# Attention order of both layers, small transfers, heads scaling, router order and the order of the last gate

## The chip, the cores and the metric

The kernel runs on one core of a Trainium2 chip. The metric is the device time of one execution in microseconds (us). Five instruction streams run beside each other on the core and meet only at semaphores: TensorE (PE, matrix products into the banks of PSUM), VectorE (DVE), ScalarE (ACT), GpSimd (POOL) and SyncE (SP). Sixteen DMA engines move data; DMAs are issued by SP, ACT and POOL, each through a queue of its own. An engine takes its instructions strictly in program order, so a wait holds back all that stands behind it on the same engine.

## The reference

A two-layer block with adaptive shifts, scales and gates, then a second block with a convolution, a linear recurrence, a router with 32 experts and a gate. 256 tokens, 1024 features, float32.

```python
def first_block(x, c, ...):
    for l in range(DEPTH):                         # 2 layers
        ada = jax.nn.silu(c) @ w_ada[l] + b_ada[l]
        sh1, sc1, g1, sh2, sc2, g2 = jnp.split(ada, 6)
        h = x * (1.0 + sc1) + sh1
        y = mixer_ab(...) if l % 2 == 0 else mixer_cd(...)
        x = layer_norm(DEEPNORM_ALPHA * x + (1.0 + g1) * y, ...)
        h = x * (1.0 + sc2) + sh2
        y = swiglu(h, w_ffn_in[l], w_ffn_out[l])
        x = layer_norm(DEEPNORM_ALPHA * x + (1.0 + g2) * y, ...)

def mixer_ab(h, ...):    # 4 heads with two softmax maps each, then 8 dilated heads
    p = softmax(s0) - lam_full * softmax(s1); oa = p @ va
    oa = oa * lax.rsqrt(jnp.mean(jnp.square(oa), -1, keepdims=True) + LN_EPS)
    oa = oa * subln_g * (1.0 - lambda_init)
    ob = dilated_attention(qb, kb, vb, ...)
    return jnp.concatenate([oa, ob], axis=-1) @ w_o

def second_block(x, p, ...):
    x = x + jnp.concatenate([y_conv, y_lru], axis=-1) @ w_out
    hf = _rmsnorm(x, g_ffn)
    eid, gate = _hier_route(hf, ...)               # best group of 4, then its 2 best of 8 experts
    x = x + _routed_experts(hf, eid, gate, w1, w3, w2)
    e = _rmsnorm(p @ w_ple, g_ple_proj)
    x = x + jax.nn.sigmoid(_rmsnorm(x, g_ple) @ w_ple_gate) * e
    return _rmsnorm(x, g_final)
```

## The kernel before

Weights of the first block and of the second one's mixers come as units of 1 MB (`w_raw`, five slots, issued by SP in order by `load_unit`, L457; each waits until PE is done with the unit five earlier). ACT splits each unit into a high part and DVE into the rest (`w_parts`, L1424 and L1971), so that a float32 product is made of three reduced ones (L740, L743, L747; in the attention L795, L797, L799). The vector `ada` comes from 48 further pieces of 1 MB (`aring`, two slots, issued by POOL, L628), each multiplied and summed on DVE in two instructions (`piece`, L1954).

The attention of a layer is eight steps j on PE: the queries and keys of step j, then `beat(j-2)`: the scores of pair j-2, the outputs of pair j-4, and the transposes of the probabilities of pair j-3 (`pair_probs`). After that come the last beats, interleaved with the output projection `from_heads`. On DVE a beat is shift (add bias, mask, minimum), the split of a unit, then the normalising of two probability tiles. In layer 0, pairs 0 to 3 are heads with two maps, whose two softmax tiles are mixed into one (`normalise`, L2076 to L2080). Their outputs land in PSUM bank 6, two heads at a time. ACT squares them (`head_squares`) and takes the root (`head_deviation`), DVE inverts it and multiplies the outputs out of PSUM (`scale_heads`, L2087 and L2090). PE transposes them (`heads_t`), ACT copies and rounds them (`take_heads`), DVE makes the rest (`heads_low`). PE waits for `head_scaled` before it writes output 2 over bank 6.

POOL's queue is in program order too: pieces, the bias bands of maps 8 to 15 (four DMAs, L652), the first row of gates written to DRAM element by element (`gate_out(0)`, L634) and read back as a row for 128 partitions (`gate_back(0)`, L638). The input `x_tm` (1 MB) is loaded by SP behind unit 13 (L504); its first use is `ln_half` (L2130). WO_AT is 12 and FF_AT is 16: units 12 to 15 are those of the output projection, 16 is the first of the feed-forward part.

The router is a chain over three engines: residual sum (L2531), multiplication by g_ffn (L2534), 16 transposes on PE (L1218), 32 products with `w_route` (L1229), then one link after another on DVE: two softmax parts, the two largest of 32, the gates (L2580 to L2589), the ranks of the tokens within their expert from five products (L1264 to L1268), the slots (L2602). Products that add zeros (`scatter`, L1247) stand between on PE. Then the 16 pairs of experts run, with 6 MB of weights each through slots in SBUF. Behind the last pair the results are scattered back (L1247), summed (L2657), transposed (L1365), and multiplied by the gate's weights `pg_parts` in four units (high parts L1377 and L1389, low parts L1382); sigmoid, product and final norm follow, and two stores of 512 KB from SP (L611).

## Time and profile before

| | us |
|---|---|
| median of 3 runs | 1271.91 |
| lowest, highest | 1270.47, 1273.64 |
| profiled execution, whole | 1268.73 |
| its span | 1266.9 |

The profile shows one execution, 3.2 us shorter than the median, with 1.8 us of its time outside the span. Times of rows are in us from the start of the span. On its axis: layer 0's attention until 144, its feed-forward part until 350, layer 1's attention 395 to 465, the mixers of the second block until 765, the router until 789, the experts until 1229, and the end. In a row of the timeline a bracket tells how long the engine was idle before it, and what ended that.

### The profile page before, as it was taken

Reading aid. Unit: us, or ns where it says so; the run is one execution under the profiler, and the core shown is the slowest. Engines: PE = TensorE matmul, PEld = TensorE weight load, DVE = VectorE, ACT = ScalarE, POOL = GpSimd, SP = SyncE. Lnnn points to the kernel's source line nnn. Section 1 sums busy time; section 2 is a strip of 40 time slices with the busy share of each in tenths; the row PEclk is TensorE's granted clock in tenths of the full one; section 3 lists DMA queues with packets and bytes.
Section 4 is the critical chain, followed back from the end, with each engine's and each line's share of the span. In section 5 each row is a group of like instructions: output and inputs, shape, how many; then the busy total and the mean of one; then the engine's idle time right before and its main releaser. Section 6 shows DMA issues by size and latency. Waiting matters only on the chain.

```text
span 1266.9 us, 16567 instructions
## 1 busy us (share of the span) xinstructions
PE 1207.7 (95%) x6608; PEld 833.4 (66%) x6608; DVE 668.0 (53%) x1194; ACT 501.1 (40%) x745; POOL 54.7 (4%) x102
## 2 busy tenths in 40 slices
PE   6997899999899999999999999999999999999987
PEld 2686678878789877888877787444544444454436
DVE  5598968687779786664468476111111111111127
ACT  1476563434475566343445375111111111111135
POOL 0111000000000000101001200000000000000000
PEclk9998999999999999999999999999999999999999
DMA  9998658988746545757556769999999999999990
GB/s 368 386 314 274 255 203 324 301 318 325 275 189 221 200 171 197 312 209 212 199 199 224 242 261 397 386 413 426 427 426 424 426 425 427 426 427 424 426 412 36
DMA packets 49035, 396.02 MB, mean 313 GB/s; under 512 B 6257, under 2 KB 7473, under 8 KB 10450
## 3 DMA queue, kind: packets, MB, share of 16 engines
q1 hardware_dynamic: 38610, 337.69, 67.7%
q0 software_dynamic: 9568, 56.55, 12.8%
q10 hardware_dynamic: 800, 0.99, 0.2%
...
## 4 chain that ended last, share of the span: by engine, by line
PE 72%; DMA 12%; DVE 10%; ACT 3%; issue 2%; SPq 1%; DVEq 0%; POOL 0%; ACTq 0%
PE psum L1295 16%; PE psum L740 9%; PE psum L747 8%; PE psum L743 8%; PE psum L1336 8%; PE psum L1239 4%; DMA slabs<-in_w 3%; DMA aring<-in_ada 3%; PE psum L1247 3%; DMA w_raw<-in_units 3%; DVE aring L1954 3%; DVE w_parts L1971 2%; DMA staged<-in_ada 2%; PE psum L795 1%; PE psum L1026 1%
## 5 line engine op out<-in xcount | busy, mean ns | idle before, releaser
L1971 DVE TENSOR_TENSOR w_parts<-w_raw,w_parts 128x2048 fp32r<-128x2048 f32 x106 | 242.1, 2288 | 92.6 <-ACT w_parts L1424 92.6
L1424 ACT ACTIVATE w_parts<-w_raw 128x2048 fp32r<-128x2048 f32 x106 | 202.0, 1911 | 104.4 <-DMA w_raw<-in_units 104.4
L1295 PE MATMUL psum<-slabs,arena 128*64 128x512 f32 x896 | 223.0, 593 | 2.8 <-issue 2.6
L740 PE MATMUL psum<-w_parts,h_parts 128*128 128x512 f32 x416 | 165.1, 397 | 4.2 <-ACT h_parts L1424 2.0
L743 PE MATMUL psum<-w_parts,h_parts 128*128 128x512 f32 x416 | 162.3, 390 | 0.0
L1295 PEld LDWEIGHTS psum<-slabs,arena 128*64 128x64 f32 x896 | 73.1, 137 | 112.1 <-issue 110.0
L1424 ACT ACTIVATE arena<-psum 128x512 f32<-128x512 f32 (+1 forms) x59 | 33.3, 567 | 272.6 <-PE psum L1309 140.9
L747 PE MATMUL psum<-w_parts,h_parts 128*128 128x512 f32 x416 | 111.5, 390 | 0.0
L1954 DVE CUSTOM_DVE_ANT_0 aring<-aring,cb 128x1024 f32<-128x1024 f32 x80 | 94.6, 1219 | 4.7 <-DMA aring<-in_ada 4.6
L740 PEld LDWEIGHTS psum<-w_parts,h_parts 128*128 128x128 f32 x416 | 78.1, 188 | 22.6 <-DVE act_tm L2167 3.4
L747 PEld LDWEIGHTS psum<-w_parts,h_parts 128*128 128x128 f32 x416 | 78.1, 188 | 16.5
L743 PEld LDWEIGHTS psum<-w_parts,h_parts 128*128 128x128 f32 x416 | 78.2, 188 | 15.5
L1938 DVE SCALAR_TENSOR_TENSOR y_lo<-psum,slot_gate,y_hi 128x512 fp32r<-128x512 f32 x32 | 24.0, 751 | 102.8 <-ACT y_hi L1424 102.8
L740 PE MATMUL psum<-w_parts,act_ring 128*128 128x512 f32 x176 | 69.6, 395 | 4.3 <-issue 2.8
L743 PE MATMUL psum<-w_parts,act_ring 128*128 128x512 f32 x176 | 69.2, 393 | 0.0
L795 PE MATMUL psum<-h_parts,w_parts 128*128 128x256 f32 x256 | 64.7, 290 | 0.0
L797 PE MATMUL psum<-h_parts,w_parts 128*128 128x256 f32 x256 | 63.2, 284 | 0.0
L1239 PE MATMUL psum<-arena,resid_tm 128*128 128x128 f32 x512 | 59.9, 275 | 0.0
L1424 ACT ACTIVATE y_hi<-psum,slot_gate 128x512 fp32r<-128x512 f32 x32 | 22.0, 687 | 93.2 <-PE psum L1336 93.2
L1239 PEld LDWEIGHTS psum<-arena,resid_tm 128*128 128x128 f32 x512 | 58.4, 192 | 0.3 <-DVE arena L2602 0.3
L1336 PE MATMUL psum<-arena,arena 128*64 128x512 f32 x256 | 56.7, 595 | 0.0
L1336 PE MATMUL psum<-w_odd,arena 128*64 128x512 f32 x256 | 56.7, 595 | 0.0
...
## 6 DMA issues: line engine op xcount, KB each, us to landing
...
```

Source lines behind the costliest of these rows:

```text
L740: mm(psum[:, bank, :], high(tile, tok), w_hi(k)[:, col:col + 512], start=first and bank not in begun, stop=False, skip_group_check=True)
L743: mm(psum[:, bank, :], high(tile, tok), w_lo(k)[:, col:col + 512], start=False, stop=False, skip_group_check=True)
L747: ins = mm(psum[:, bank, :], low(tile, tok), w_hi(k)[:, col:col + 512], start=False, stop=done, skip_group_check=True)
L795: mm(half(j % 2, s), w_hi(k)[:, at_(kt)], h_hi[:, kt, :], start=kt == 0 and s == 0, stop=False, skip_group_check=True)
L797: mm(half(j % 2, s), w_lo(k)[:, at_(kt)], h_hi[:, kt, :], start=False, stop=False, skip_group_check=True)
L1239: last = nc.tensor.matmul(psum[:, bank_no, k * P:(k + 1) * P], hf_t(t, kt), hot_s[:, t, :, :], start=t == 0, stop=t == TT - 1)
L1247: last = nc.tensor.matmul(psum[:, 4 + 2 * t + c, :], hot_gt[:, t * P:(t + 1) * P], part[:, c * 512:(c + 1) * 512], start=start and n == 0, ...
L1295: ins = nc.tensor.matmul(psum[s * CAP:(s + 1) * CAP, w, :], xe_t[:, kt, s * CAP:(s + 1) * CAP], up_weights(w, s, b, kt), start=kt == 0, st ...
L1336: ins = nc.tensor.matmul(psum[s * CAP:(s + 1) * CAP, c, :], act_t[:, f, s * CAP:(s + 1) * CAP], w2_at[b][:, c * 4096 + s * 2048 + f * 512: ...
L1424: return nc.scalar.activation(out_ap, in_ap, func, **kw)
L1954: v.tensor_tensor_reduce(out=w, in0=w, in1=cb[:], scale=1.0, scalar=0.0, op0=ALU.mult, op1=ALU.add, accum_out=ada_raw[:, 2 * slot + t:2 * ...
L1971: v.tensor_tensor(w_lo(k), raw(k), w_hi(k).bitcast(F32), ALU.subtract).then_inc(w_split, 1)
```

## The change

Both layers' attention: on PE the transposes of the probabilities of pair j-3 move from the inside of the beat to behind the products of step j; on ACT the copies of these tiles move with them. In layer 0 each head's output gets a half bank of its own in banks 6 and 7, and the output of head 2 no longer waits for `head_scaled`; the first transposes of heads move from beat 4 to behind step 6. DVE only inverts the roots (`head_factors`); ACT multiplies the heads (`scale_heads`). The mix of two maps is written with one map left without its own denominator, and the root takes a bias per head and token, which makes four roots of one column out of one of four. The bands of maps 8 to 15, `gate_out(0)` and `gate_back(0)` are issued by ACT, and POOL issues pieces 8 to 21 without anything between. `x_tm` is loaded behind unit 17. In both layers pairs 4 and 5 are rounded on ACT ahead of exponentials.

Router: g_ffn is multiplied into `w_route` earlier in the program; PE transposes the sum itself; the five products for the ranks read rounded operands (`tri_r`, `ones_r`, `both_r`); ahead of them stand 8 wide and 16 narrow products with zeros, where 24 wide ones stood; the gates are computed after the slots and after the number of rounds is signalled.

End: half of the last scatter moves into the last expert's second products, high and low parts of the gate's products are interleaved differently, DVE makes all four halves of the sum before the low weights, and spreads the latter between the low parts of the sum; the table for the sigmoid is loaded earlier, the one for the last root without a call of its own; the last chunk is squared on DVE; ACT stores tile 0.

```diff
@@ SP
-                if k == WO_AT + 1:
+                if k == FF_AT + 1:
                     sp.dma_start(x_tm[:], a["x_rows"]).then_inc(x_in, 16)
@@ POOL
             bands(0, 4)
-            pieces(8, 10)
-            pieces(10, 12)
-            pool.wait_ge(bias_in, BANDS)
-            bands(8, 16)
-            pieces(12, 14)
-            gate_out(0)
-            pieces(14, 16)
-            gate_back(0)
-            pieces(16, 22)
+            pieces(8, 22)
@@ PE, attention
-                if i == 2:
-                    pe.wait_ge(head_scaled, 1)
-                elif i:
+                if i % 2:
                     pe.wait_ge(head_squared, i)
...
+                    if j >= 3:
+                        pair_probs(layer, j - 3)
+                    if layer == 0 and j == 6:
+                        heads_t(0)
@@ PE, router
-            for _ in range(3):
-                for c in range(2):
-                    scatter(c, True, False)
-
-            pe.wait_ge(route_d, 3)
+            for c in range(2):
+                scatter(c, True, False)
+            for n, part in enumerate((y_hi, y_lo)):
+                for k in range(8):
+                    nc.tensor.matmul(psum[:, 4 + k // 4, k % 4 * P:k % 4 * P + P], hot_gt[:, 0:P], part[:, k * P:(k + 1) * P],
+                                     start=False, stop=False, skip_group_check=True)
+
+            pe.wait_ge(route_d, 2)
@@ ACT, attention
+            def scale_heads(n):
+
+                act.wait_ge(head_rooted, head_rooted_from + n + 1)
+                for i in (2 * n, 2 * n + 1):
+                    for t in range(TT):
+                        col = head_col(i, t)
+                        ins = A(o_tm[:, i, t, :], head_bank(i)[:, t * P:(t + 1) * P], Cp, scale=head_sq[:, 2, col:col + 1])
+                ins.then_inc(head_scaled, 1)
...
+            def first_gate_back():
+                act.wait_ge(first_gate, first_gate_from + 16)
+                act.dma_start(g_row[:], bass.AP(gate_rows.tensor, 0, [[0, P], [1, D]])).then_inc(first_gate, 16)
...
                     split(u + QK_AT + j + 3)
+                    if layer == 0 and j == 5:
+                        scale_heads(0)
+                    if layer == 0 and j == 2:
+                        bands(8, 16)
+                    elif layer == 0 and j == 7:
+                        first_gate_out()
@@ DVE, normalise of a head with two maps
-                    link(v.reciprocal(den[:, m0:m + 1, :], den[:, m0:m + 1, :]))
-                    link(v.tensor_scalar(den[:, m, :], den[:, m, :], small[:, 14:15], None, ALU.mult))
-                    v.tensor_scalar(s1[:, 0:256], s1[:, 0:256], den[:, m, 0:1], None, ALU.mult)
-                    link(v.tensor_scalar(s1[:, 256:384], s1[:, 256:384], den[:, m, 1:2], None, ALU.mult))
-                    stt(s[:, 0:256], s[:, 0:256], den[:, m0, 0:1], s1[:, 0:256], ALU.mult, ALU.add)
+                    stt(head_sq[:, 3, m0:m0 + 2], den[:, m0, :], LN_EPS, den[:, m0, :], ALU.mult, ALU.mult)
+                    link(v.reciprocal(den[:, m, :], den[:, m, :]))
+                    link(stt(den[:, m, :], den[:, m, :], small[:, 14:15], den[:, m0, :], ALU.mult, ALU.mult))
+                    stt(s[:, 0:256], s1[:, 0:256], den[:, m, 0:1], s[:, 0:256], ALU.mult, ALU.add)
@@ DVE, heads
-            def scale_heads(n):
+            def head_factors(n):
 
                 dve.wait_ge(head_std, n + 1)
-                link(v.reciprocal(head_sq[:, 2, 4 * n:4 * n + 4], head_sq[:, 1, 4 * n:4 * n + 4]))
-                for i in (2 * n, 2 * n + 1):
-                    for t in range(TT):
-                        ins = v.tensor_scalar(o_tm[:, i, t, :], psum[:, 6, (i % 2) * T + t * P:(i % 2) * T + (t + 1) * P],
-                                              head_sq[:, 2, 2 * i + t:2 * i + t + 1], None, ALU.mult)
-                ins.then_inc(head_scaled, 1)
+                v.reciprocal(head_sq[:, 2, 4 * n:4 * n + 4], head_sq[:, 1, 4 * n:4 * n + 4]).then_inc(head_rooted, 1)
@@ DVE, router: the gates' operations (nine) move behind this line
+            v.tensor_copy(rounds_i[:], r_s[:, 12, 0:1]).then_inc(routed, 2)
@@ DVE, end
             summed(0, 0)
+            summed(1, 0)
+            gate_low(0, 0)
             summed(0, 1)
-            gate_low(0, 0)
+            summed(1, 1)
+            pg_low(0)
             gate_low(0, 1)
-            pg_low(0)
             pg_low(1)
-            summed(1, 0)
-            summed(1, 1)
             pg_low(2)
@@ ACT, end
+            table_of_sigmoid()
...
-            table_of_sqrt()
             token_root("final", 0)
```

PE in layer 0's attention, before: the scores of a pair (L822), the output of head 2 (L875 to L877), the transposes of scaled heads (L884), the transposes of probabilities (L840 to L842).

```order
L822 MATMUL psum<-qk 128x256 [waits qk_taken,score_rd]
L822 MATMUL psum<-qk 128x256
L822 MATMUL psum<-qk 128x128 x2
L875 MATMUL psum<-val,prob_t 128x128 [waits head_scaled,pt_copied]
L876 MATMUL psum<-val,prob_t 128x128
L877 MATMUL psum<-val,prob_t 128x128
L884 MATMUL psum<-cst,o_tm 128x128 [waits head_scaled]
L884 MATMUL psum<-cst,o_tm 128x128 x3
L840 MATMUL psum<-cst,score 128x128 [waits pt_copied,prob_ready]
L841 MATMUL psum<-cst,score 128x128
L842 MATMUL psum<-cst,score 128x128
```

The same place after, from the last row of the scores on; L803 and L805 are the products of step 6:

```order
L830 MATMUL psum<-qk 128x128 x2
L879 MATMUL psum<-val,prob_t 128x128 [waits pt_copied]
L880 MATMUL psum<-val,prob_t 128x128
L881 MATMUL psum<-val,prob_t 128x128
L803 MATMUL psum<-h_parts,w_parts 128x256
L805 MATMUL psum<-h_parts,w_parts 128x256
```

PE after, at the end of step 6, with the transposes of probabilities (L848 to L850) and of heads (L888):

```order
L805 MATMUL psum<-h_parts,w_parts 128x256
L807 MATMUL psum<-h_parts,w_parts 128x256 x8
L848 MATMUL psum<-cst,score 128x128 [waits pt_copied,prob_ready]
L849 MATMUL psum<-cst,score 128x128
L850 MATMUL psum<-cst,score 128x128
L888 MATMUL psum<-cst,o_tm 128x128 [waits head_scaled]
L888 MATMUL psum<-cst,o_tm 128x128 x3
L803 MATMUL psum<-h_parts,w_parts 128x256 [waits qk_taken,w_split]
```

The output of head 2 lost its wait for `head_scaled`, and both kinds of transposes moved from the beat to behind step 6's products, the heads behind the probabilities.

ACT in layer 0's attention, before, from the last `take_qk` to the last exponentials (line 1424 is the helper of all activations):

```order
L1424 ACTIVATE qk<-psum 128x512
L1424 ACT_TABLE_LOAD
L1424 ACTIVATE head_sq<-head_sq,small 128x4
L1424 ACTIVATE w_parts<-w_raw 128x2048
L1424 ACTIVATE o_whole<-psum,small 128x512
L1424 ACTIVATE o_parts<-o_whole 128x512
L1424 ACT_TABLE_LOAD
L1424 ACTIVATE score,den<-score,mins 128x256
```

ACT after, the same place (helper in line 1449):

```order
L1449 ACTIVATE qk<-psum 128x512
L1449 ACTIVATE prob_t<-psum 128x384 x2
L1449 ACT_TABLE_LOAD
L1449 ACTIVATE head_sq<-head_sq 128x1 x4
L1449 ACTIVATE o_tm<-psum,head_sq 128x128 x4
L1449 ACTIVATE w_parts<-w_raw 128x2048
L1594 DMA gate_rows<-drv 128x8x1
L1449 ACTIVATE o_whole<-psum,small 128x512
L1449 ACTIVATE o_parts<-o_whole 128x512
L1449 ACTIVATE o_parts<-psum 128x256
L1449 ACT_TABLE_LOAD
L1449 ACTIVATE score,den<-score,mins 128x256
```

PE at the end, before, from the last expert's second products (L1336) to the transposes of the sum (L1365); `y_hi` and `y_lo` are the parts of the last expert's result:

```order
L1336 MATMUL psum<-w_odd,arena_81 64x512 x7
L1354 REGISTER_ALU
L1247 MATMUL psum<-y_hi,hot_gt 128x512 [waits y_low0,sgt_c]
L1247 MATMUL psum<-y_lo,hot_gt 128x512
L1247 MATMUL psum<-y_hi,hot_gt 128x512
L1247 MATMUL psum<-y_lo,hot_gt 128x512
L1247 MATMUL psum<-y_hi,hot_gt 128x512 [waits y_low1]
L1247 MATMUL psum<-y_lo,hot_gt 128x512
L1247 MATMUL psum<-y_hi,hot_gt 128x512
L1247 MATMUL psum<-y_lo,hot_gt 128x512
L1365 MATMUL psum<-cst,x_tm 128x128 [waits x_ready]
L1365 MATMUL psum<-cst,x_tm 128x128 x3
```

PE after, the same place:

```order
L1359 MATMUL psum<-w_odd,arena_81 64x512 [waits w2_loaded11]
L1359 MATMUL psum<-w_odd,arena_81 64x512 x3
L1356 REGISTER_ALU
L1264 MATMUL psum<-y_hi,hot_gt 128x512 [waits y_low0,sgt_c]
L1264 MATMUL psum<-y_hi,hot_gt 128x512
L1264 MATMUL psum<-y_lo,hot_gt 128x512 [waits y_low0]
L1264 MATMUL psum<-y_lo,hot_gt 128x512
L1359 MATMUL psum<-w_odd,arena_81 64x512 x4
L1381 MATMUL psum<-cst,x_tm 128x128 [waits x_ready,y_low0]
L1381 MATMUL psum<-cst,x_tm 128x128 x3
L1259 REGISTER_ALU
L1264 MATMUL psum<-y_hi,hot_gt 128x512 [waits y_high]
```

Four scatter products moved into the second products (L1359), and the first transposes (L1381) ahead of the other four.

## Rows read from the trace of the kernel before

**Rows 1.** The page: span, and busy tenths of PE in 40 slices.

```profile
span 1266.9 us, 16567 instructions
...
PE   6997899999899999999999999999999999999987
```

**Rows 2.** The page: the chain that ended last, shares by engine.

```profile
PE 72%; DMA 12%; DVE 10%; ACT 3%; issue 2%; SPq 1%; DVEq 0%; POOL 0%; ACTq 0%
```

**Rows 3.** Timeline of PE, layer 0's attention: start, busy us, line, what, idle before.

```profile
99.66 0.76 PE L875 MATMUL psum<-val,prob_t 128*128 128x128 f32 x2 [5.07 <-DVE o_tm L2090]
```

**Rows 4.** Windows there: busy us (instructions) of PE, PEld, DVE, ACT, POOL; clock, DMA share, GB/s.

```profile
102.00:104.00 2.00, 2.00 (x12) 2.00 (x11) 1.54 (x4) 2.00 (x9) 0.00 (x0) 0.55 0.10 8
104.00:106.00 2.00, 2.00 (x19) 2.00 (x19) 1.76 (x4) 1.37 (x4) 0.00 (x0) 1.00 0.89 57
...
136.00:138.00 2.00, 2.00 (x13) 1.72 (x12) 1.97 (x4) 1.94 (x4) 0.53 (x1) 1.00 0.00 0
```

**Rows 5.** Timeline of DVE, layer 0's attention and the start of its norm.

```profile
93.90 1.23 DVE L1954 CUSTOM_DVE_ANT_0 aring<-aring,cb 128x1024 f32<-128x1024 f32 x1 [1.62 <-DMA aring<-in_ada]
...
96.86 0.35 DVE L2078 TENSOR_SCALAR score<-score,den 128x256 f32<-128x256 f32 x1
...
98.39 1.13 DVE L2090 TENSOR_SCALAR o_tm<-psum,head_sq 128x128 f32<-128x128 f32 x4
...
109.91 0.42 DVE L2059 CUSTOM_DVE_ANT_0 score<-psum,bias 128x256 f32<-128x256 f32 x1 [2.48 <-PE psum L822]
...
132.74 0.42 DVE L2102 TENSOR_TENSOR o_parts<-psum,o_parts 128x256 fp32r<-128x256 f32 x1 [1.64 <-ACT o_parts L1424]
...
144.43 0.68 DVE L2130 TENSOR_TENSOR ln_tmp<-psum,g_row 128x512 f32<-128x512 f32 x1
```

**Rows 6.** Timelines of ACT and POOL, and landing times of the DMAs on the gates' rows.

```profile
130.57 0.51 ACT L1424 ACTIVATE score<-score,mins 128x256 f32<-128x256 f32 x1 [3.42 <-DVE mins L2061]
...
74.65 2.36 POOL L652 DMA_DIRECT2D bias<-bias_rows  x4
...
DMA to landing us min/median/max: 8.9/10.0/14.1
```

**Rows 7.** Timeline of SP: unit 17's issue; landing times of the weights from 100 to 160.

```profile
139.24 0.33 SPq L461 DMA_DIRECT2D w_raw<-in_units  x1
...
DMA to landing us min/median/max: 4.7/7.4/12.4
```

**Rows 8.** Timeline of PE, layer 1's attention.

```profile
439.61 0.47 PE L740 MATMUL psum<-w_parts,o_parts 128*128 128x512 f32 x1 [0.73 <-issue]
```

**Rows 9.** Timelines of PE and DVE in the router.

```profile
771.18 1.26 PE L1218 MATMUL psum<-cst,resid_tm 128*128 128x128 f32 x8 [1.11 <-DVE resid_tm L2534]
...
788.89 4.51 PE L1295 MATMUL psum<-slabs,arena 128*64 128x512 f32 x20
...
781.59 0.16 DVE L2580 TENSOR_REDUCE arena<-arena 128x2 f32<-128x8 f32 x1
...
783.56 0.20 DVE L2591 TENSOR_SCALAR arena<-arena 128x64 f32<-128x64 f32 x1
```

**Rows 10.** The chain in the last experts, and a window in the first.

```profile
1188.73 22.34 DMA slabs<-in_w
...
792.00:794.00 2.00, 2.00 (x12) 0.67 (x10) 0.00 (x0) 0.00 (x0) 0.00 (x0) 1.00 0.76 250
```

**Rows 11.** Timelines of PE, DVE, ACT and SP at the end.

```profile
1234.80 1.16 PE L1377 MATMUL psum<-pg_parts,g_hi 128*128 128x512 f32 x4 [1.26 <-ACT pg_parts L1424]
...
1235.93 4.87 DVE L1938 SCALAR_TENSOR_TENSOR pg_parts<-slabs,vec,pg_parts 128x1024 fp32r<-128x1024 f32 x4
...
1258.96 1.28 ACT L1424 ACT_TABLE_LOAD   x1
1260.26 0.20 ACT L1424 ACTIVATE small<-small 128x1 f32<-128x1 f32 x1
...
1262.55 0.82 SPq L611 DMA_DIRECT2D out<-resid_tm  x2
```

373 lines of the change are left out of this document (214 added, 159 removed).

## The prediction

> **What bounds the kernel now.** I read the page first: PE is busy in nearly every slice [rows 1], and the chain of waits is 72% PE, with 12% DMA and 10% DVE [rows 2]. So an edit pays only where PE, or what it waits for, comes late on that chain. The timeline then says where. In layer 0's attention the chain runs through DVE: PE stood 5.07 us before it could write output 2, because DVE was still scaling heads [rows 3], and came back at a low clock. From 102 to 104 the granted clock was 0.55 and PE did 12 instructions; in the next 2 us, at 1.00, it did 19 [rows 4]. DVE itself had few gaps: 1.62 us on a piece, 2.48 on scores, 1.64 on ACT [rows 5]. Its last link is the start of the first norm at 144.43 [rows 5]. Layer 1's attention has one gap worth the name, 0.73 us [rows 8]. In the router PE waits 1.11 us for the gain, and the first expert product starts at 788.89 [rows 9]. The last experts end on DMAs: 22.34 us of chain for one slab [rows 10]. The end is PE, then a table load, a root and two stores from one queue [rows 11].
>
> **Layer 0's attention.** What DVE loses: four scalings of heads, 1.13 us, twice, with the reciprocals staying, so 2.26 us; and in each of four mixes one pass of 0.35 us over a tile, 1.4 us in all [rows 5]. That is 3.7 us off an engine that is on the chain. What the freed PE gains is more, 5.07 us and about 1.5 us of half clock (23 instructions in 4 us of which 19 fit into 2 us, less what the clock gave back), but PE then runs into DVE. I carried this through: scores of pair 5 move from 109.91 to about 102, since the gap of 2.48 and part of the 1.62 go with PE's stall; behind them the lead shrinks, because DVE now works without a gap and waits for roots and for ACT's scaled heads instead. ACT's four scalings have a cover: ACT was idle 3.42 us in one place of this stretch [rows 6]. The norm starts 4.2 us earlier by this, just above the 3.7 us. The bounds: 1.0, if DVE meets new waits for nearly all that it lost, and 9.4, if the 3.7 us and all three gaps (5.74 us) go.
>
> Against it stands `x_tm`. SP now issues it behind unit 17, whose issue came at 139.24 [rows 7]. That issue waits for PE, so it moves with the lead to 135.0, and `x_tm` follows at about 135.4. The norm would need it at 140.2. The DMA engines had a hole from 136 to 138 [rows 4], and the weights of this stretch landed after 4.7 us at best, 7.4 in the middle, 12.4 at worst [rows 7]. The best gives 140.1 and no wait, the middle 142.8 and 2.6 us, the worst 147.8 and 7.6 us. I take 1.0, nearer the best because of the hole. Before, `x_tm` was loaded long ahead and cost nothing.
>
> **Small transfers.** Four bands, which took POOL 2.36 us to issue [rows 6], now take ACT's time behind the split of step 2. There ACT waited for DVE, so I price them at nothing; without that cover it is 2.4 us. `gate_out(0)` is issued at about 114 and lands 8.9 to 14.1 us later [rows 6], at 123 to 128. ACT reaches the wait for it at about 123, and its next exponentials would be free at 126.4 (130.57 less 4.2), so its idle 3.42 us hide a landing up to 12.4 us after issue. The worst row leaves 1.7 us. Queued behind that wait are the rounding of pair 5 and two tiles' exponentials, for which DVE and PE wait. I take 0.3. POOL's pieces no longer stand behind these transfers, but the piece that DVE waited 1.62 us for was held by its free slot and its landing, so I give the move nothing. The stage's sum is 4.2 - 1.0 - 0.3 = 2.9 us, between -5.7 (the lead at 1.0, `x_tm` at its middle, bands and gates uncovered) and 9.4.
>
> **Layer 1's attention.** The order of transposes fills the gap of 0.73 us [rows 8]; DVE loses nothing here. 0.5 us, between 0 and 1.
>
> **Router.** PE's 1.11 us before the second transposes go, since the gain is off the chain; I take 1.0. The nine linked gate operations between 781.59 and 783.56 [rows 9], 1.97 us, leave the way to the slots, but PE's products for the ranks stand there too, so that about 1.4 us come through. The first expert product moves from 788.89 to 786.5, 2.4 us. It is not worth that at the end: the experts end on DMAs [rows 10], so only what fills the dip in the first of them counts. From 792 to 794 the DMA engines were busy 0.76 of the time [rows 10], so about 0.5 us of transfer was missed there. An earlier start of the experts shortens that hole and what lies beside it. I take 1.2, between 0.5 and 2.4.
>
> **End.** Scatter products inside the second products take away the shadow in which nothing else was ready; PE's 1.26 us before the gate's first product [rows 11] shrink by half. But DVE must now make four sums, four low parts of the sum and eight passes of 1.22 us over low weights (4.87 us for four [rows 11]) without a gap: 8 passes over 512 columns at 0.68 [rows 5] and 9.7 us are 15.1 us from about 1232, so the last low weights are there at 1247, where PE asks for them. I take 0.7 us of loss on PE. Behind the last product the table load of 1.28 us [rows 11] starts 0.3 us earlier, and the stores, issued 0.4 us apart by one queue (0.82 us for both [rows 11]), come from two queues together: 0.5 us of gain. Sum: -0.2 us, between -1.5 and 1.5.
>
> Table loads have a second price. On the chain at the end, ACT's table load took 1.28 us, and the next activation started 0.02 us behind it [rows 11]. The Trainium skill ("ScalarE: Activation LUTs", "What ACT_TABLE_LOAD costs") adds a drain of 1.38 us to each switch. By the page, hiding the loads of the router and of the sigmoid would give 2.8 us more, and the sum would be 7.2 us; the trace shows no drain, and I go by the trace.
>
> **Sum.** 2.9 + 0.5 + 1.2 - 0.2 = 4.4 us. The profiled execution took 1268.73 us, so it would take 1264.3. The median is 3.2 us above the profiled execution; the forecast is 1267.5. A measurement of this kernel can tell about 0.3%, 3.8 us, from no change, that is less than 1268.1 is faster and more than 1275.7 slower.
>
> **Rivals.**
> Forecast, 0.50: DVE's lost work comes through, 1263.5 to 1270.
> More, 0.17: the gaps of DVE go with its work. Layer 0 gives 9.4 - 1.3 = 8.1, layer 1 0.5, the router its whole 2.4, the end 0: 11.0 us, 1260.9. For it: PE's stall was the cause of the 2.48. Against: each gap has a different releaser, and DMAs end the experts.
> DVE stays the clock, 0.20: PE's idle time only moves, from output 2 to the wait for `prob_ready`, since the transposes now stand ahead of step j+1; layer 0 gives 1.0, the router 0.5, the end costs 0.5: 1.0 us, 1270.9. This is also how it would look if the order did not do what it says.
> Late `x_tm`, 0.13: at its worst landing, the first norm starts at 147.8, 3.4 us later than before, and PE stands for that time, as all of DVE's queue is behind that wait. With 0.5, 1.2 and -0.2 of the others that is 1.9 us slower, 1273.8. It decides from a landing of 9.0 us after issue: then the norm starts where it did.
>
> **How the numbers follow.** The likeliest case gives 1267.5. The range 1260.5 to 1273.5 leaves out about half of the last rival, the low side of the second, and little of the others, under 2 in 10. Faster by over 0.3%: 0.42 of the forecast's 0.50 and the second's 0.17, 0.59. Slower: 0.10, the last rival with a transfer later than seen, or a stage at its lower bound. Same: the rest, 0.31.
>
> **What would show it.** Right: no idle time of PE on scaled heads; clock 1.00 from 100 to 104; first norm at 140 to 142; first expert product at 786 to 787; last product of the gate about 1 us later than the shift of the rest. Wrong: an idle DVE before the norm that ends on `x_tm`; ACT idle on the gates' rows ahead of exponentials; PE idle on low weights at the end; a first expert product 2.4 us nearer and an end that gained it all.

## The result and the profile after

| | before | after |
|---|---|---|
| median of 4 runs each, us | 1271.85 | 1263.93 |
| lowest, highest | 1270.47, 1273.64 | 1262.62, 1265.41 |
| profiled execution, whole | 1268.73 | 1264.81 |
| its span | 1266.9 | 1263.0 |

The ratio of the medians is 0.9933, with a 95% interval from 0.9911 to 0.9956: 7.9 us faster. The two profiled executions differ by 3.9 us only. Before's lies 3.1 us below its median, after's 0.9 above its own. So the profiles can place a gain, but they can't be summed to the medians. The experiments show later why.

The page of the kernel after: its span, the busy tenths of PE, and the shares of the chain. They answer to [rows 1, 2].

```profile
span 1263.0 us, 16569 instructions
...
PE   6998899999899999999999999999999999999987
...
PE 74%; DMA 11%; DVE 9%; ACT 3%; issue 1%; SPq 1%; DVEq 0%; POOL 0%; ACTq 0%
```

PE's share of the chain rose from 72% to 74%; DMA and DVE each lost a point.

**Layer 0's attention.** Timelines of PE and DVE after, four rows with idle time from 60 to 142 us. They answer to [rows 3, 5].

```profile
108.42 0.77 PE L748 MATMUL psum<-w_parts,o_parts 128*128 128x512 f32 x1 [2.47 <-issue]
...
135.66 0.79 PE L755 MATMUL psum<-w_parts,o_parts 128*128 128x512 f32 x1 [2.23 <-DVE o_parts L2172]
...
123.54 0.43 DVE L2172 TENSOR_TENSOR o_parts<-psum,o_parts 128x256 fp32r<-128x256 f32 x1 [2.20 <-ACT o_parts L1449]
...
139.69 0.69 DVE L2200 TENSOR_TENSOR ln_tmp<-psum,g_row 128x512 f32<-128x512 f32 x1 [1.89 <-PE psum L755]
```

The stall of 5.07 us before output 2 is gone, and no PE row waits for a scaled head. About half of it came back at another place: at 108.42 PE waits 2.47 us before the first product of the output projection. The view names no releaser, but this product waits for `qk_taken` (L905), and ACT's last copy of queries and keys ended at 108.32. That copy stands in ACT's order behind exponentials, and ACT had been idle 2.89 us for DVE's minima ahead of them. In the experiments below this wait is there with 2.46 to 2.48 us in every kernel that has the attention of the change without an edit. At 135.66 PE waits another 2.23 us for the low part of a head's output on DVE. The first norm starts at 139.69 instead of 144.43, 4.7 us earlier. The windows of 2 us of the kernel after, with the columns of [rows 4]:

```profile
102.00:104.00 2.00, 2.00 (x19) 2.00 (x19) 1.97 (x6) 0.72 (x5) 0.53 (x1) 1.00 0.40 168
...
108.00:110.00 2.00, 1.58 (x4) 1.32 (x5) 1.93 (x7) 1.98 (x4) 0.00 (x0) 0.50 0.91 356
...
136.00:138.00 2.00, 2.00 (x6) 1.52 (x6) 1.80 (x1) 1.82 (x1) 0.10 (x1) 0.50 1.05 438
...
160.00:162.00 2.00, 2.00 (x6) 1.62 (x5) 1.80 (x2) 2.00 (x5) 1.73 (x4) 0.50 0.19 49
```

The last three columns are clock, DMA share and GB/s. From 102 to 104 the clock is 1.00, as predicted. But it is 0.50 at three other places, the first of them right behind the wait of 2.47 us; it may fall there in one execution and not in the next (below). From 136 to 138 the DMA engines are now full, where before they stood still [rows 4].

**`x_tm` and the gates' row.** Timelines of SP and ACT after, with the landing time of `x_tm`. They answer to [rows 6, 7].

```profile
131.55 0.43 SPq L522 DMA_DIRECT2D x_tm<-in_x_rows  x1
...
DMA to landing us min/median/max: 8.1/8.1/8.1
...
111.49 0.39 ACTq L1594 DMA_DIRECT2D gate_rows<-drv  x1
...
123.13 0.38 ACT L1449 ACTIVATE o_parts<-psum 128x256 fp32r<-128x256 f32 x1 [1.45 <-DMA gate_rows<-drv]
```

`x_tm` was issued at 131.55 and its landing was seen 8.1 us later, at 139.65. The norm starts there. The view puts DVE's 1.89 us down to PE, but that product had ended at 138.94; the last 0.7 us are the transfer's. The norm also waits for `x_tm` in every other execution whose `x_tm` stands behind unit 17, eleven in the experiments below: it landed 8.1 or 8.2 us after its issue in all of them, and the norm started within 0.1 us of the landing. DVE was idle 1.9 to 2.0 us there, and PE's product had ended 0.7 to 2.2 us before. It had ended late in the execution above, since the clock was 0.50 from 136 to 138. So 0.7 us is the low end of what the transfer costs. ACT waits 1.45 us for the gates' row, and behind it DVE waits the 2.20 us for `o_parts` shown above.

**Router.** PE after: transposes, ranks, first expert product, against [rows 9].

```profile
766.74 2.20 PE L1221 MATMUL psum<-cst,x_tm 128*128 128x128 f32 x16
...
777.81 0.28 PE L1284 MATMUL psum<-both_r,tri_r 128*128 128x32 f32 x1 [1.74 <-DVE both_r L2649]
...
783.22 1.08 PE L1315 MATMUL psum<-slabs,arena 128*64 128x512 f32 x4
```

The transposes begin 2.3 us earlier than before (769.04), the first expert product 5.7 us earlier than in [rows 9]. So the router gained 3.4 us in this pair of traces, a pair in which the clock fell behind the transposes before and not after. All of it arrives: the second products of the last expert pair start at 1216.50 instead of 1222.24, 5.7 us earlier. The DMAs at [rows 10] didn't hold it back.

**End.** PE and DVE after, behind the last second products, and a window of the same place. They answer to [rows 11].

```profile
1225.67 0.75 DVE L2015 SCALAR_TENSOR_TENSOR y_lo<-psum,slot_gate,y_hi 128x512 fp32r<-128x512 f32 x1 [3.94 <-ACT y_hi L1449]
1226.34 1.27 DVE L2729 TENSOR_TENSOR x_tm<-x_tm,psum 128x512 f32<-128x512 f32 x2
1227.17 0.72 PE L1381 MATMUL psum<-cst,x_tm 128*128 128x128 f32 x4 [2.26 <-DVE x_tm L2729]
...
1228.00:1230.00 2.00, 2.00 (x6) 1.54 (x6) 1.45 (x3) 2.00 (x3) 0.00 (x0) 0.50 0.41 168
...
1253.58 1.12 PE L1405 MATMUL psum<-pg_parts,g_hi 128*128 128x256 f32 x8
```

Here is a new wait. PE transposes the sum of the first half, and that sum stands in DVE's order behind the low part of the second half of `y`, which comes late: PE is idle 2.26 us and then has the low clock. From the start of the second products to the end of the gate's last product it takes 38.2 us (1216.50 to 1254.70), before 35.8 us (1222.24 to 1258.04). Behind the last product the rest takes 8.3 instead of 8.9 us. Timelines of ACT and SP there:

```profile
1255.22 1.28 ACT L1449 ACT_TABLE_LOAD   x1
1256.52 0.48 ACT L1449 ACTIVATE rms<-rms,small 128x1 f32<-128x1 f32 x2
...
1258.60 0.37 ACTq L2000 DMA_DIRECT2D out<-resid_tm  x1
...
1258.60 0.34 SPq L628 DMA_DIRECT2D out<-resid_tm  x1
```

The two stores now leave together.

### The profile page after: what moved, and what is told of

Read it like the earlier page. It is cut to its first block, busy times and chain, and to the rows that moved or that the text cites. A ratio compares the mean times of both kernels' runs of the same rounds, so it can differ in the third digit from the quotient of the medians.

```text
span 1263.0 us, 16569 instructions
## 1 busy us (share of the span) xinstructions
PE 1207.7 (96%) x6603; PEld 834.0 (66%) x6603; DVE 665.2 (53%) x1185; ACT 506.3 (40%) x761; POOL 51.1 (4%) x96
## 3 DMA queue, kind: packets, MB, share of 16 engines
q0 software_dynamic: 9072, 54.97, 12.5%
q10 hardware_dynamic: 3216, 3.10, 1.0%
## 4 chain that ended last, share of the span: by engine, by line
PE 74%; DMA 11%; DVE 9%; ACT 3%; issue 1%; SPq 1%; DVEq 0%; POOL 0%; ACTq 0%
PE psum L1315 16%; PE psum L748 8%; PE psum L751 8%; PE psum L755 8%; PE psum L1359 8%; PE psum L1243 4%; DMA slabs<-in_w 3%; DMA w_raw<-in_units 2%; PE psum L1251 2%; PE psum L803 2%; DMA staged<-in_ada 2%; PE psum L807 2%; PE psum L805 2%; DVE w_parts L2048 2%; DMA gate_rows<-drv 2%; DVE aring L2031 2%
## 5 line engine op out<-in xcount | busy, mean ns | idle before, releaser
L803 PE MATMUL psum<-h_parts,w_parts 128*128 128x256 f32 x256 | 64.8, 291 | 0.0
L805 PE MATMUL psum<-h_parts,w_parts 128*128 128x256 f32 x256 | 62.6, 282 | 0.0
L1359 PE MATMUL psum<-w_odd,arena 128*64 128x512 f32 x256 | 56.9, 596 | 0.0
L1359 PE MATMUL psum<-arena,arena 128*64 128x512 f32 x256 | 56.7, 595 | 0.0
## 6 DMA issues: line engine op xcount, KB each, us to landing
w_odd<-in_w SPq DMA_DIRECT2D x16, 1024.0 KB, 19.9
```

The costliest lines, as they stand in the source:

```text
L803: mm(half(j % 2, s), w_hi(k)[:, at_(kt)], h_hi[:, kt, :], start=kt == 0 and s == 0, stop=False, skip_group_check=True)
L805: mm(half(j % 2, s), w_lo(k)[:, at_(kt)], h_hi[:, kt, :], start=False, stop=False, skip_group_check=True)
L1359: ins = nc.tensor.matmul(psum[s * CAP:(s + 1) * CAP, c, :], act_t[:, f, s * CAP:(s + 1) * CAP], w2_at[b][:, c * 4096 + s * 2048 + f * 512: ...
```

## The experiments

The runs form three groups (e1 to e4, e5 to e8, e9 to e12), each with its own runs of the kernel before. The medians of these were 1273.61 (1268.64 to 1279.18), 1270.33 (1267.27 to 1272.94) and 1270.43 (1265.14 to 1276.33), with 17, 17 and 19 runs. Microseconds are compared within a group, and across groups only as ratios to the kernel before. Behind a median stand the lowest and the highest run, behind a ratio its 95% interval.

### The changed kernel again (e1), and its parts undone (e2 to e4)

The first is the changed kernel without an edit.

> The changed kernel itself once more, as the base for the three beside it. Path theory (each stage's lead reaches the end): 0.993 to 0.995 of before. Chance theory (before's profiled execution at 1268.73 is typical and the other four were slow ones): 0.996 to 0.998. Its trace tells whether the drops of the granted clock at 108, 135, 159, 347 and 1227 us come again at the same places; if they do, they belong to the order and not to one execution.

Measured: 1263.61 (1262.51 to 1268.58), ratio 0.9924 [0.9902, 0.9946]. That is the base of this group. Its profiled execution was its slowest, with a span of 1266.8. Windows of it, in layer 0 and in the router:

```profile
112.00:114.00 2.00, 2.00 (x7) 1.21 (x6) 1.44 (x6) 1.74 (x6) 0.00 (x0) 0.61 0.98 410
...
780.00:782.00 2.00, 2.00 (x7) 1.61 (x7) 1.71 (x10) 0.00 (x0) 0.00 (x0) 0.50 0.99 426
...
786.78 5.80 PE L1315 MATMUL psum<-slabs,arena 128*64 128x512 f32 x26
```

The last row is the first expert product of this execution. The same program came there at 786.78 instead of 783.22. It was 0.8 us behind at the router's transposes (767.52 against 766.74). The other 2.8 us lie behind the ranks, where the clock was 0.5 from 778 to 784 and the execution above had 1.00. Three of the five drops came again, at the same work: those at 108, 136 and 1228 stand at 112, 140 and 1232 here, as this execution was 2.5 us later from the first scores on. Those at 160 and 348 didn't.

The end of before, in a kernel that is otherwise the changed one:

```diff
-                        if last and c == 1 and f == 2:
-                            pe.wait_ge(sgt_c, n_all + 1)
-                            last_scatter(0)
...
             summed(0, 0)
+            summed(0, 1)
+            gate_low(0, 0)
+            gate_low(0, 1)
+            pg_low(0)
+            pg_low(1)
             summed(1, 0)
-            gate_low(0, 0)
-            summed(0, 1)
             summed(1, 1)
-            pg_low(0)
-            gate_low(0, 1)
-            pg_low(1)
             pg_low(2)
...
-            act.dma_start(out[:, 0, :], resid[:, 0, :]).then_inc(stored, 16)
```

> Changed kernel with the end of before (scatter, sums, gate products, final norm and stores as before; attention and router changed). Theory A, from the two traces: the end lost 1.8 us (12.56 to 12.89 us up to the gate's first product, 23.3 to 25.3 us for the gate's products, 0.5 us gained behind them), so this runs 1.5 to 2 us below the changed kernel, and the drop of the clock at 1227 is gone. Theory B, the prediction's: the end is worth nothing, within 0.5 us of the changed kernel.

Measured: 1261.93 (1261.55 to 1263.97), 0.9912 [0.989, 0.9934], 1.7 us faster than e1. So by the medians the new end costs 1.7 us, where the forecast had it cost 0.2; the intervals overlap. First row of its last second products and the last one of the gate:

```profile
1217.47 4.94 PE L1343 MATMUL psum<-w_odd,arena 128*64 128x512 f32 x22
...
1252.15 1.12 PE L1396 MATMUL psum<-pg_parts,g_hi 128*128 128x256 f32 x8
```

That is 35.8 us, the length of before, against 38.2 us in the profile after. The loss sits in this stretch.

The router of before, in a kernel that is otherwise the changed one (transposes of the sum multiplied by the gain, 24 wide zero products, ranks from the two-hot tile behind all gate operations):

```diff
-                    pe.wait_ge(x_ready, 4 + 2 * t + c + 1)
+                    pe.wait_ge(normed, 16 + 2 * t + c + 1)
...
-            hot_m = both_r
+            hot_m = r_both
```

> Changed kernel with the router of before. Theory A: the router's 3.3 us (transposes 3.24 to 2.03, zero products 7.16 to 5.55, ranks 2.12 to 1.65) reach the end in full, 3 to 4 us above the changed kernel, first expert product at about 786.5. Theory B, the prediction's: DMAs end the experts, so no more than 1.2 us of it arrives at the end, while the first expert product is still 3 us later.

Measured: 1265.6 (1264.34 to 1266.63), 0.9939 [0.9917, 0.996], 2.0 us slower than e1: the router's part is worth 2.0 us by the medians, between what the two theories said. Its PE rows show the wait for the gain again:

```profile
767.35 1.26 PE L1222 MATMUL psum<-cst,resid_tm 128*128 128x128 f32 x8 [1.10 <-DVE resid_tm L2591]
```

The attention of before, small transfers and scaling of heads with it, with the router and the end of the change:

```diff
-                if k == FF_AT + 1:
+                if k == WO_AT + 1:
                     sp.dma_start(x_tm[:], a["x_rows"]).then_inc(x_in, 16)
...
-                    if j >= 3:
-                        pair_probs(layer, j - 3)
-                    if layer == 0 and j == 6:
-                        heads_t(0)
...
-                if i % 2:
+                if i == 2:
+                    pe.wait_ge(head_scaled, 1)
+                elif i:
```

> Before, with the router and the end of the change alone (attention of both layers, transfers, x_tm as before). Theory A: the attention gained 4.7 us up to the first norm and kept 1.4 to 2.5 us of it up to the router, so this runs about 2 us above the changed kernel. Theory B: it kept everything in most executions (the drop of the clock at 159 is one execution's), so 4.5 to 5.5 us above.

Measured: 1270.88 (1267.71 to 1273.88), 0.9984 [0.9967, 1.0001], 7.3 us slower than e1, more than either theory said. Nearly the whole gain is in the attention. PE stands before output 2 again, and the norm is as late as before:

```profile
99.28 0.46 PE L892 MATMUL psum<-val,prob_t 128*128 128x128 f32 x2 [2.49 <-DVE o_tm L2147]
...
145.96 0.69 DVE L2187 TENSOR_TENSOR ln_tmp<-psum,g_row 128x512 f32<-128x512 f32 x1
```

The three parts sum to 7.3 + 2.0 - 1.7 = 7.6 us. The medians differ by 7.9 us in the first comparison and 10.0 in this group. A ratio's interval is 0.22% to either side here, 2.8 us, so the sum fits both, and none of the three is known better than to a microsecond or two.

### What of the attention's part did it (e5, e6, e10)

The small transfers back on POOL, at their old places among the pieces:

```diff
-            pieces(8, 22)
+            pieces(8, 10)
+            pieces(10, 12)
+            pool.wait_ge(bias_in, BANDS)
+            bands(8, 16)
+            pieces(12, 14)
+            gate_out(0)
+            pieces(14, 16)
+            gate_back(0)
+            pieces(16, 22)
```

> Changed kernel with the bands of maps 8 to 15, gate_out(0) and gate_back(0) issued by POOL between its pieces again, as before. Queue theory (the move off POOL made the attention's gain): 3 to 5 us above the changed kernel's 1263.6. Order theory (the order on PE and the heads made it): within 1 us of it, since the trace showed ACT waiting 1.45 us for the gates' rows, which this gives back.

Measured: 1273.31 (1269.52 to 1276.59), 1.0026 [1.0013, 1.0038]. The changed kernel stands at 0.9924, 0.9928 and 0.9933 in its three measurements, so this costs some 12 us, far beyond the 3 to 5 expected, and the kernel is slower than before. Timelines of POOL and DVE, and two windows:

```profile
96.86 0.91 POOL L650 DMA_DIRECT2D gate_rows<-drv  x1 [10.55 <-DVE drv L2056]
97.76 0.54 POOL L645 DMA_DIRECT2D aring<-in_ada  x1
...
116.01 1.23 DVE L2033 CUSTOM_DVE_ANT_0 aring<-aring,cb 128x1024 f32<-128x1024 f32 x1 [12.34 <-DMA aring<-in_ada]
...
102.00:104.00 2.00, 2.00 (x20) 1.88 (x17) 1.64 (x5) 1.54 (x5) 0.03 (x1) 1.00 0.92 37
...
110.00:112.00 2.00, 0.00 (x0) 0.00 (x0) 0.00 (x0) 0.00 (x0) 0.00 (x0) 0.62 1.02 426
```

The piece that DVE needs next was issued at 97.76, 0.9 us behind the gates' row. It landed 18.2 us later. The DMA engines were 0.92 busy with 37 GB/s, and from 108 to 116 no engine computed. Part of the 12 us is an interaction: DVE now takes its pieces in another order than before, and the old order of POOL's queue fits that worse than the old DVE. In the kernel before, the same pair of transfers was issued at 98.57 and 99.47, and the piece landed after 14.0 us, but nothing waited for it. So the slow landing alone cost nothing there, and that the transfers cost 12 us in the kernel before isn't shown.

The Trainium skill ("DMA: Bandwidth & Descriptors", "Issuing engines are not separate DMA queues") says that starting DMAs on several engines saves only the sequencer's time to start them, "which is usually small relative to the DMA itself". By that, the move would be worth no more than the issues themselves, 2.36 us for the four bands [rows 6] and 0.91 us for the gates' row, off an engine that computes nothing. The run disagrees: 12 us hung on which queue the transfers stood in. POOL waited 10.55 us for the gates' row's operand with the piece standing behind it. How the 12 us divide between this and the slow landing behind the row isn't shown.

Heads scaled and maps mixed on DVE as before, the order and all else of the change kept:

```diff
-                v.reciprocal(head_sq[:, 2, 4 * n:4 * n + 4], head_sq[:, 1, 4 * n:4 * n + 4]).then_inc(head_rooted, 1)
+                link(v.reciprocal(head_sq[:, 2, 4 * n:4 * n + 4], head_sq[:, 1, 4 * n:4 * n + 4]))
+                for i in (2 * n, 2 * n + 1):
+                    for t in range(TT):
+                        col = head_col(i, t)
+                        ins = v.tensor_scalar(o_tm[:, i, t, :], head_bank(i)[:, t * P:(t + 1) * P],
+                                              head_sq[:, 2, col:col + 1], None, ALU.mult)
+                ins.then_inc(head_scaled, 1)
```

> Changed kernel with the heads scaled on DVE and the two maps mixed as before (2.3 and 1.4 us of DVE work back), order and banks as changed. If DVE's work was the attention's gain: 3 to 4 us above 1263.6, first norm about 3.5 us later. If the order was (output 2 no longer waits for scaled heads, 5.07 us of idle PE): 1 us or less.

Measured: 1262.65 (1260.5 to 1265.65), 0.9946 [0.9929, 0.9962]. Its interval holds one of the changed kernel's three ratios and lies 0.0001 and 0.0005 above the others. By its ratio the changed kernel would stand at 1261.2 us in this group (0.9928 of 1270.33), 1.4 us lower. The window from 60 to 140 of before, after and this kernel, one row each in this order, then the first norm of this kernel:

```profile
60.00:140.00 80.00, 69.02 (x497) 60.83 (x495) 71.19 (x191) 51.96 (x122) 9.15 (x16) 0.94 0.80 269
```

```profile
60.00:140.00 80.00, 72.69 (x514) 62.90 (x514) 70.18 (x183) 59.01 (x140) 5.84 (x11) 0.96 0.90 287
```

```profile
60.00:140.00 80.00, 72.17 (x513) 62.82 (x512) 73.94 (x194) 55.36 (x126) 5.81 (x11) 0.96 0.85 285
...
140.10 0.69 DVE L2201 TENSOR_TENSOR ln_tmp<-psum,g_row 128x512 f32<-128x512 f32 x1 [1.98 <-issue]
```

DVE has its 3.7 us of work again (73.94 against 70.18 us busy), and the norm comes 0.4 us later than after's. DVE did more work than before in the same 80 us, 73.94 against 71.19: it had idle time before, and the change let it be used. The work does reach PE on the way: its wait before the output projection is 4.80 us in this execution, until 110.16, against 2.47 us. Most of that is made up again up to the norm. So most of DVE's lost work was not what moved the norm; that it is worth 1 or 2 us isn't excluded.

The wait before output 2 alone put back:

```diff
-                if i % 2:
+                if i == 2:
+                    pe.wait_ge(head_scaled, 1)
+                elif i % 2:
                     pe.wait_ge(head_squared, i)
```

> Changed kernel in which PE waits for the scaled heads 0 and 1 again before it writes output 2, which is the wait that held PE 5.07 us before. Order theory (that wait was worth 4 us of the attention's gain): 3 to 5 us above the base, and an idle PE there. Rival (with the heads scaled earlier, on ACT, nobody waits): within 0.5 us of the base.

Measured: 1263.86 (1260.29 to 1270.97), 0.9959 [0.9938, 0.998], beside 1261.1 of the changed kernel in the same group (e9, below): 2.8 us, just under the 3 to 5 expected. Timeline of PE, one window, and the first norm:

```profile
97.11 0.77 PE L881 MATMUL psum<-val,prob_t 128*128 128x128 f32 x2 [2.28 <-ACT o_tm L1451]
...
98.00:100.00 2.00, 2.00 (x11) 2.00 (x11) 2.00 (x5) 1.24 (x7) 0.00 (x0) 0.50 0.67 168
...
142.61 0.69 DVE L2202 TENSOR_TENSOR ln_tmp<-psum,g_row 128x512 f32<-128x512 f32 x1 [1.90 <-issue]
```

PE stands 2.28 us and has half the clock from 96 to 102, and in exchange the wait of 2.47 us before the output projection is gone. The norm comes 2.9 us later than after's 139.69. But 1.5 us of that were there before the wait (the scores ahead of it start at 93.91 here and at 92.43 after), and e1, which has no such wait, has its norm at 142.49. Counted from the first scores of the same execution to the norm, this kernel takes 78.8 us and the changed one 76.0 to 77.7. So a wait of PE was passed on to the norm, though DVE had 3.7 us less to do than in the kernel before; the trace gives it 1 to 3 us.

### The element-wise transfer (e7)

Each gates' row was a column of 128 partitions by 8 values, written to DRAM as 1024 elements of 4 bytes. Here it is written as 128 runs of 32 bytes. The features of the gates then stand in another order, so this kernel applies each gate to the wrong feature; the number and size of all other operations stay.

```diff
-                    pool.dma_start(bass.AP(gate_rows.tensor, q * D, [[1, P], [P, KT]]), drv[:, q, 0, :]).then_inc(g_out, 16)
+                    pool.dma_start(bass.AP(gate_rows.tensor, q * D, [[KT, P], [1, KT]]), drv[:, q, 0, :]).then_inc(g_out, 16)
...
-                    act.dma_start(bass.AP(gate_rows.tensor, 0, [[1, P], [P, KT]]), drv[:, 0, 0, :]).then_inc(first_gate, 16)
+                    act.dma_start(bass.AP(gate_rows.tensor, 0, [[KT, P], [1, KT]]), drv[:, 0, 0, :]).then_inc(first_gate, 16)
```

> Changed kernel, with all four transfers of gates to DRAM written as 32 B runs in place of 4 B elements; the gates' features are then in another order, so that is left out of what is computed. While such a transfer was on its way (about 10 us each), the other queues moved 27 to 30 GB/s in the feed-forward part of layer 0, and ACT waited 6.7 us for a weight. Theory A, the elements hold the DMA engines and cost time behind it: 1 to 3 us below 1263.6, landing of the gates' rows about 2 us instead of 10. Theory B, the queues are deep enough: no difference within 0.5 us.

Measured: 1259.04 (1257.18 to 1261.29), 0.9915 [0.9899, 0.993], some 2 us below the changed kernel's 1261.2 in this group. The intervals overlap, but the trace says the same: from the first norm of layer 0 to the second it takes 195.8 us (139.72 to 335.51), and 198.0 to 200.1 us in the eight executions with the whole new attention. For the changed kernel: landing times of the four rows and their way back, and a window in layer 0's feed-forward part. Then the same of this kernel.

```profile
DMA to landing us min/median/max: 5.7/10.0/13.0
...
224.00:226.00 2.00, 2.00 (x13) 1.69 (x11) 1.89 (x3) 0.60 (x1) 0.00 (x0) 1.00 0.85 29
```

```profile
DMA to landing us min/median/max: 2.4/4.1/4.9
...
224.00:226.00 2.00, 2.00 (x10) 1.66 (x9) 2.00 (x4) 1.74 (x3) 0.00 (x0) 1.00 0.98 414
```

4 KB in elements of 4 bytes keep the DMA engines 0.85 busy at 29 GB/s, and everything else waits behind them. The landing times are those of the writes and of their ways back together. The Trainium skill ("DMA: Bandwidth & Descriptors", "Rules for kernel authors") says that a non-contiguous last dimension becomes one descriptor per element, and advises to rearrange it. The packet counts of the profile agree for the row that ACT issues: its queue had 3216 packets after and 2320 in this kernel, fewer by 896, which is 1024 elements less 128 runs. For POOL's three rows they show nothing, since its queue has 9072 packets in both.

### The end (e8, e9, e11), and the clock (e12)

Eight wide products more behind the last second products, of which nothing is used:

```diff
             second_products(1, rounds * (PAIRS // 2 * 16), last=True)
+            for _ in range(8):
+                nc.tensor.matmul(psum[:, 2, :], hot_gt[:, 0:P], y_hi[:, 0:512], start=True, stop=True, skip_group_check=True)
```

> Changed kernel with eight products of 512 columns more, into a bank that nobody reads, behind the last expert's second products, where PE was idle 2.26 us and the clock then fell to 0.50 for 2 us. Clock theory: the clock stays at 1.00 from 1226 to 1232, and the kernel is 1 to 1.4 us below 1263.6. Rival (the idle time is set by DVE's second y_lo alone, and the clock matters to nothing that is late): no difference, or up to 0.3 us more where the eight end behind the sum.

Measured: 1260.8 (1257.06 to 1263.17), 0.9925 [0.9909, 0.9942], not told apart from the changed kernel. In the trace the clock holds:

```profile
1225.45 0.63 PE L1383 MATMUL psum<-cst,x_tm 128*128 128x128 f32 x4 [0.19 <-DVE x_tm L2731]
...
1228.00:1230.00 2.00, 2.00 (x12) 1.65 (x12) 2.00 (x4) 1.42 (x3) 0.00 (x0) 1.00 0.08 31
```

The idle time of 2.26 is 0.19, and the stretch from second products to the gate's last product is 36.8 us against 38.2. But that is one execution, and the expected 1 to 1.4 us aren't in the median. The changed kernel once more, beside e10 to e12:

> The changed kernel once more, as the base of the three beside it: 1261 to 1264 us.

Measured: 1261.1 (1258.48 to 1263.2), 0.9928 [0.9905, 0.9951]; its profiled execution had a span of 1256.7. Windows of this execution:

```profile
146.00:148.00 2.00, 2.00 (x9) 1.96 (x10) 1.86 (x9) 0.51 (x1) 0.27 (x1) 0.50 0.71 295
...
1228.00:1230.00 2.00, 2.00 (x9) 1.48 (x9) 2.00 (x3) 2.00 (x3) 0.00 (x0) 1.00 0.00 0
```

From the start of the second products (1211.46) to the gate's last product (1248.29) it takes 36.8 us. PE waited the same 2.26 us for the sum as in the profile after, but the clock held. So the order costs 1.0 us against the 35.8 of before, and the clock 1.4 us more where it falls. The filling of e8 gave no more than a clock that held by itself.

The changed tail with the order of before ahead of it: the kernel of e2, but table loads, last norm and stores as in the change:

```diff
-            pe.wait_ge(y_low[0], n_all + 1)
-            gate_tiles(0, 0)
-            last_scatter(1)
-            gate_high(0, 0, first)
...
+            gate_tiles(0)
+            for j in range(4):
+                gate_high(0, j, first)
```

> Changed kernel with the end of before up to the gate's last product, and only what follows it changed (sigmoid, square of the last chunk, root, two stores from two queues). From the traces: 35.8 us from the last second products to the last gate product in place of 38.2, and 8.3 us behind it in place of 8.9. So 2 to 3 us below the base. If the tail's 0.5 us were chance: 1.7 us below, as with the whole end undone.

Measured: 1260.2 (1258.76 to 1261.17), 0.9919 [0.9896, 0.9942], 0.9 us below e9. I had expected 2 to 3 us. Its stretch is 35.8 us (1212.93 to 1248.74), 1.0 to 2.4 us shorter than with the new order. But behind the gate's last product it takes 9.4 us, against 8.3 in the profile after and 8.9 before. ACT reads that product only 1.1 us after its end, and the chain of this execution is ACT and DVE alone from 1240 on, with a table load of 1.28 us in it. So the gain of the tail didn't come together with the old order, and it took back 1.0 us of what the order gave. It has the lowest median of this group; whether it beats the changed kernel isn't settled, as the intervals overlap.

The kernel of e11 with nine transposes of the identity put before each norm's last transposes, to keep PE going there:

```diff
+                    if t and q < 3 and c == 0:
+                        pe.wait_ge(ln_whole, 4 * q + 1)
+                        for _ in range(9):
+                            nc.tensor.transpose(psum[:, 6, 0:P], ident, ident)
```

> The kernel beside it with nine transposes of a constant into the bank that is next, ahead of the second half of each of the three norms, where PE is idle 1.6 us and the clock fell to 0.50 in some executions (at 159 and 347 us). Clock theory: no drop behind the norms in its trace, 0.5 to 1.5 us below the kernel beside it, with a narrower spread. Rival (PE is not idle long enough, the nine delay the norm's transposes): up to 0.5 us above it.

Measured: 1262.27 (1257.51 to 1266.76), 0.9932 [0.9907, 0.9956], 2.1 us slower than e11, more than the rival had said, at nearly the same span of the profiled execution (1258.2 and 1258.1); the intervals overlap. PE at the second norm of layer 0:

```profile
353.25 1.15 PE L928 MATMUL psum<-cst 128*128 128x128 f32 x9
354.23 1.36 PE L937 MATMUL psum<-cst,resid_tm 128*128 128x128 f32 x8
```

The transposes ran in the gap ahead of the norm's second half and closed it, and nothing was gained. Whether short gaps at the norms feed the clock drops isn't settled by this. That gap was 0.8 us in e11; the one of 1.65 us ahead of the first half stayed as it was. And e11's trace had no drop behind a norm that the transposes could have prevented.

### The same stretches in all executions

A single trace misleads where the clock may fall or not. The table gives stretches of all fourteen profiled executions, each between two rows of the same execution, in us; in brackets how many.

| | as before | changed, clock held | changed, clock fell |
|---|---|---|---|
| first scores to first norm of layer 0 | 82.2 and 83.4 (2) | 76.0 to 77.7, with and without a drop (9) | |
| router's transposes to first expert product | 19.8 and 19.9 (2) | 16.5 (6) | 17.9 to 19.5 (6) |
| last second products to the gate's last product | 35.8 (4) | 36.8 (4) | 38.2 (5) |

The first row leaves out e5, e6 and e10, which take 89.6, 77.8 and 78.8 us; the last leaves out e8. In the router "fell" means a drop behind the ranks. On average the router gives 2.3 us and the new order of the end costs 1.8, of which its tail gives back 0.5. The experts between, from the first product to the last second products, take 433.4 and 434.2 us with the old router and 431.6 to 433.5 with the new one.

One part of the attention's gain can be placed without a run of its own. Before, PE waited for a mixed tile of DVE inside a beat:

```profile
71.41 0.33 PE L840 MATMUL psum<-cst,score 128*128 128x128 f32 x1 [1.41 <-DVE score L1938]
```

From the second scores to the third it took 8.5 us there (10.5 in e4), and 7.1 in all executions with the transposes behind the products, e6 among them, which mixes as before. So the place of the transposes is worth 1.4 us here.

## Why the prediction was right, and where not

The forecast was 1267.5, the median 1263.9, within the range and on the side of faster. The ratio was forecast at 0.9965 and measured at 0.9933. The sum of 4.4 us was too small, and its main step had the wrong cause. That the range held is in part luck: the attention and the router gave more than forecast, the end took more. All four signs that were named for "wrong" came in some form: an idle DVE that ends on `x_tm`, ACT idle on the gates' row, PE idle on low weights (0.32 us), and an end that gained all of the router's lead.

**Layer 0, the step that failed.** The prediction let the norm move by "DVE's lost work" of 3.7 us, rounded up to 4.2. The size of the move was near: 4.7 us in the two traces. Over the eight executions of kernels with the whole new attention (e7 and e10 aside) the norm starts at 138.1 to 142.5, mean 139.8; over the two with the old one at 144.43 and 145.96, mean 145.2. That is 5.4 us, and 5.8 counted from the first scores. The cause was for the most part another. Against the mean of 77.0 us from the first scores to the norm, DVE's work put back (e6) costs 0.9 us and the wait put back (e10) 1.9; the medians give 1.4 and 2.8. The place of the transposes gives 1.4. These are single executions beside a spread of 1.7 us, so their order is shown better than their sizes. DVE's queue held idle time and waits that gave way as soon as PE stopped stalling. Of the rivals, "more" had this mechanism: PE's stall was the cause of DVE's gaps. I gave it 0.17 and its price was too high, 8.1 us in layer 0. "DVE stays the clock" was half right as well: of PE's idle time 2.47 us only moved, though not to the wait for `prob_ready` but to that for the last queries and keys. PE's busy time from 60 to 140 us grew by 3.7 us, not by the 5.07 of the stall. The scores of pair 5 came to DVE at 105.30 and not at about 102. The result lies between the forecast and "more".

**Small transfers, a term put at nothing.** "the piece that DVE waited 1.62 us for was held by its free slot and its landing, so I give the move nothing." This held for the queue before. In the changed kernel the move is what makes the new order of pieces possible (e5, 12 us). For the gates' row I took 0.3 us; ACT was idle on it 1.45 us, and DVE 2.20 behind it. What that cost the norm isn't shown: in e7, where the wait is gone, the stretch from the first scores to the norm is 76.0 us, at the low end of the others'. The landing of 11.2 us lay within the rows' 8.9 to 14.1.

**`x_tm`.** Forecast 135.4 for the issue and 1.0 us of wait. It was issued at 131.55, landed after 8.1 instead of 4.7 us, and cost 0.7 us in the profile after. Over the eight executions with the whole new attention it was 0.7 to 2.0 us, 1.5 on average: the norm's start is the landing of `x_tm` in every one. The step leaned on the hole in the DMA engines from 136 to 138 [rows 4]; there was none, since DMAs issued earlier filled it (438 GB/s). That SP came to the issue 4 us earlier than I had it made up for the slow landing, and that was luck. No run loads `x_tm` earlier with all else as changed, so whether the 1.5 us can be had is open. The late-`x_tm` rival put its turning point at 9.0 us after an issue at 135.4, that is a landing at 144.4; the measured landing at 139.65 is far from it.

**Clock.** 1.00 from 100 to 104 was right, and so was that PE's stall had lowered it there: with the wait put back the clock is at 0.50 there again. The prediction didn't say that a drop may turn up at another place. After had them at 108, 136 and 160. The one at 108 follows the new wait of 2.47 us, and came in six of the nine executions that have this wait.

**Layer 1.** Forecast 0.5 us, between 0 and 1. From the second norm of layer 0 to the first of layer 1 it took 121.5 us before (341.66 to 463.15) and 120.9 after. Over the same executions as above the gain of this stretch is 1.0 us, the upper bound.

**Router, a term mis-sized.** Forecast 1.2 us of 2.4, since "the experts end on DMAs". Measured 2.0 us by e3, 3.4 us in the two traces, and 2.3 us on average over the executions of the table: 3.4 where the clock holds behind the ranks, 0.3 to 1.9 where it falls. The failed step is the discount. I took a link of DMA on the chain near the end [rows 10] for a bound of all experts. After, no window of 2 us from 786 to 796 is below 397 GB/s, the dip was gone, and the 5.7 us of lead at the first expert product were 5.7 at the last.

**End, mis-sized and misplaced.** Forecast -0.2: 0.7 lost on PE, 0.5 gained in the tail. The tail gave 0.5 to 0.6, as forecast. PE lost 1.0 us by the order and 1.4 more where the clock falls, in five of nine executions; the median gives -1.7. The place was wrong too. I looked for low weights late at the end of the gate; PE waited 0.32 us on them. The wait was at the front, where the first transposes stand behind a sum that DVE takes up only after the low part of `y`.

**Table loads.** As in [rows 11] the activation behind ACT's last table load starts 0.02 us after it (1255.22 and 1.28 us of load, then 1256.52). The Trainium skill's drain of 1.38 us ("ScalarE: Activation LUTs", "What ACT_TABLE_LOAD costs") is not seen after either, and the sum that went by the trace was the right one to use here; that the sum of 7.2 us by the Trainium skill is nearer to 7.9 is no support for the drain.

**The last step, from the profile to the median.** I added 3.2 us as the median stands above the profiled execution. The profiled execution of before lay at the low end of its spread: 17 executions in the first group of experiments ran from 1268.64 to 1279.18, and 1268.73 is at the bottom. Nothing says that the changed kernel's would lie there too. That is why the traces differ by 3.9 us and the medians by 7.9.

What stays open: how the 5.4 us of layer 0 divide exactly between the lost wait, the place of the transposes, the order of the pieces and the place of the transfers, since these need each other; what `x_tm` takes from them; and whether DVE's scaling costs up to 2 us in the median (e6's interval allows it) or nothing.
